# Seven products in both halves of the FFN down columns, two buffers for the weight sums, and PSUM halves copied by ScalarE

## The chip, the cores and the metric

The kernel runs on one core of a Trainium2 chip. The metric is the device time of one execution in microseconds (us). The kernel before takes 1904.34 us, the median of three runs (1903.96 to 1905.06 us).

## The reference, cut to what matters

Two encoder layers over 256 positions of width 2048. Each has a mixing part (projection, dilated attention, pooling, output projection) and a feed-forward part; the change is in the second:

```python
f = jnp.square(jax.nn.relu(rms_norm(x, g_ffn_pre) @ w_up)) @ w_down
return x + rms_norm(f, g_ffn_post)
```

`w_up` is 2048 x 8192, `w_down` 8192 x 2048, all in f32.

## The kernel before

**Products.** TensorE takes fp32r operands, so every f32 operand is split into a high part (a cast, on ScalarE) and a low part (operand minus high part, on VectorE), and a product is three matmuls: high x high, high x low, low x high (`three`, lines 845 to 849, whose three matmuls are L847, L848, L849). ScalarE makes `w_hi` (`split_hi`, L956), VectorE `w_lo` (`split_lo`, L1356). Weights come as 0.5 MB pieces into the four buffers `raw` (SP's queue issues the load of a buffer once its `w_lo` is made), and the split pieces lie in a ring of eight slots (`RING`). A slot is written again after TensorE has used it (`w_used`).

**The FFN.** A layer has four groups `g`, each of 2048 of the 8192 hidden columns: four up units (`turned_unit`, hidden by position, so that the results are already laid out for the down product), then two wide down stages, `j` = 0 for output columns 0 to 1023 and `j` = 1 for 1024 to 2047. The last group of a layer does the second half in two narrow units instead (`unit`). A wide stage goes through 16 blocks of 128 hidden rows, in `K_ORDER`; a block has four products (two halves of the positions t, two halves of the columns c), which add up in the four banks of `acc_pair`.

**Seven products.** In stage `j` = 0 four pairs of blocks (`SEVEN_AT`: blocks 0, 4, 8 and 12) take seven products for eight, by Strassen's scheme (`seven`, L851). It needs sums of quarters of the activations (`s_sum`, `s_hi`, `s_lo`, made while the up units run) and of the weights (`t_sum`, `t_hi`, `t_lo`: in `seven_lo`, L1892, four subtractions of 128x512, two `w_lo`, one `t_lo` of 128x1536, two `w_lo`). Four of the seven results (`ssa_bank`, both `t_bank`, `o_bank`) are shared by several outputs. They add up in PSUM over all four groups and are added to `acc` once in a layer (`combine`, L1921). `t_sum` has one buffer, so that VectorE begins the sums of the next pair when TensorE has used those of this one (`t_used`).

**Moving results.** After a wide stage VectorE adds its four banks to `acc` (`wide_sums`, L1855; L1843 in the first group, L1846 after). After each half of an up unit (`b` = 0 is complete three quarters into the unit, `b` = 1 at its end) VectorE adds the two 256-column halves of a bank (`turned_square`: a reduction at L1822), then does maximum and square (L1827); ScalarE casts `f_hi` (L1248), VectorE makes `f_lo` (L1833).

**Order.** Each engine's instructions run in the order in which the program writes them; the order of VectorE around the down stages is that of `wide_pair` (L1952) and `group` (L1969), the order of ScalarE that of its own `turned_unit` (L1266) and `group` (L1287). TensorE waits for `acc_free` before the first product into a bank, for `lo_made` before a slot, for `t_lo_made` before the products with weight sums.

Of the kernel before, what the change touches and what calls it, by code (L numbers as in the profile page):

```python
# [141 lines left out]
K_ORDER = ((4, 5, 0, 1, 6, 7, 2, 3, 8, 9, 12, 13, 10, 11, 14, 15), tuple(range(2 * RING)))  # L142


def seven_no(l, g, n):

    return (l * FF_GROUPS + g) * len(SEVEN_AT) + n
# [13 lines left out]
def build(nc, x_in, positions, g_mix_pre, w_in, g_attn_out, w_pool, pool_scale, g_pool_out,  # L161
# [16 lines left out]
    x = own("x", [P, T, D])  # L178
# [50 lines left out]
    q_sum = at("q_sum", [P, 4, CH], F32, r_h)  # L229
    raw_side = at("raw_side", [P, RAW, 2 * CH], F32, r_h + 16384)  # L230
    t_hi = at("t_hi", [P, 3, CH], F32R, r_qkv + 12 * CH)
    t_sum = at("t_sum", [P, 3, CH], F32, r_qkv + 24 * CH)
    t_lo = at("t_lo", [P, 3, CH], F32R, r_qkv + 24 * CH)
# [6 lines left out]
    bias = own("bias", [P, T, SEQ])  # L240
    over_count = own("over_count", [P, len(WINDOWS), SEQ])
# [65 lines left out]
    p_copied, q_step = sem("p_copied"), sem("q_step")  # L307
# [60 lines left out]
    with nc.Block() as block:  # L368
# [3 lines left out]
        def _(sp):  # L372
# [33 lines left out]
            def load_wide(l, g, j, hu):  # L406

                for i in range(SLOTS):
                    p = i % PAIRS

                    sp.wait_ge(lo_made, (hu + i // PAIRS) * PAIRS + p + 1)
                    src = w_down[ld(l, 1), ld(g * D + K_ORDER[j][i] * P, P), ld(j * 2 * CH, 2 * CH)]
                    sp.dma_start(raw[:, p, :], src.rearrange("a p c -> p (a c)")
                                 ).then_inc(raw_loaded[p], 16)
# [81 lines left out]
        def _(pe):  # L496
# [163 lines left out]
            for l in range(DEPTH):  # L660
# [190 lines left out]
                def seven(g, n, hu, result):  # L851

                    i = SEVEN_AT[n]
                    no, s0, s1 = seven_no(l, g, n), i % RING, i % RING + 1
                    k0, k1 = K_ORDER[0][i], K_ORDER[0][i + 1]
                    first = n == 0
                    p_first = first and isinstance(g, int) and g == 0
                    p_last = isinstance(g, int) and g == FF_GROUPS - 1 and n == len(SEVEN_AT) - 1
# [3 lines left out]
                    pe.wait_ge(flo_made, l * 32 + g * 8 + k1 // 2 + 1)  # L862
                    pe.wait_ge(s_lo_made, no + 1)
                    pe.wait_ge(lo_made, (hu + i // PAIRS) * PAIRS + 2 + RAW)
                    three(ssa_bank[:, :], sh[:, 2, :], sl[:, 2, :], w_hi[:, s0, right],
                          w_lo[:, s0, right], p_first, p_last)
                    three(t_bank[0][:, :], f_hi[:, k0, early], f_lo[:, k0, early], w_hi[:, s0, left],
                          w_lo[:, s0, left], p_first, p_last).then_inc(w_used, 1)
# [6 lines left out]
                    pe.wait_ge(t_lo_made, no + 1)  # L875
                    three(t_bank[1][:, :], sh[:, 0, :], sl[:, 0, :], t_hi[:, 0, :], t_lo[:, 0, :],
                          p_first, p_last).then_inc(t_used, 1)
                    three(o_bank[:, :], sh[:, 1, :], sl[:, 1, :], t_hi[:, 1, :], t_lo[:, 1, :],
                          p_first, p_last).then_inc(t_used, 1)
                    if first:  # L880
                        pe.wait_ge(acc_free[1], result + 1)
                    three(acc_pair[1][:, 0, :], f_hi[:, k1, late], f_lo[:, k1, late],
                          t_hi[:, 2, :], t_lo[:, 2, :], first, False).then_inc(t_used, 1)

                def down_wide(g, j, hu, result):

                    for i in range(SLOTS):
                        slot, kt = i % RING, K_ORDER[j][i]
# [7 lines left out]
                        for t in range(T):  # L896
                            for c in range(2):
                                if i == 0:
                                    pe.wait_ge(acc_free[t], result + c)
                                begin = i == 0 if j else i == 2 and (t, c) == (1, 1)  # L900
# [1371 lines left out]
```

## Time and profile before

| | |
|---|---|
| median of the runs | 1904.34 us |
| profiled execution, span | 1903.1 us |
| TensorE busy | 1891.0 us, 99% |
| VectorE busy | 1445.1 us, 76% |
| ScalarE busy | 983.1 us, 52% |
| DMA: share of 16 engines, bytes | 62%, 381 MB |
| largest groups of VectorE and ScalarE | `w_lo` 832.3 us, `w_hi` 705.5 us |

The profile is of one execution: its span of 1903.1 us runs from the first to the last instruction, 1.2 us below the median of the runs. A matmul row gives the time until its result has drained, so two neighbours overlap; what a matmul costs TensorE is the distance between two starts. Rows of VectorE and ScalarE overlap a little in the same way.

### The profile page before, as it was taken

How to read it: one execution, taken by the hardware profiler on the slowest of the kernel's cores; microseconds unless marked ns; L12 is line 12 of the kernel's file. 1: busy time of each engine (PE TensorE's matmuls, PEld its weight loads, DVE VectorE, ACT ScalarE, POOL GpSimd, SP SyncE). 2: the span in 40 equal slices, each digit the busy share in tenths (PEclk: the TensorE clock that was granted, in tenths of full speed). 3: DMA queues.
4: the chain of work that ended last, by engine and by line, in shares of the span. 5: the costliest groups of instructions: out<-in, count | busy, mean ns of one | idle time of the engine just before them, and what ended most of it. 6: DMA issues, size and time to landing. Idle time of an engine off the chain costs nothing.

```text
span 1903.1 us, 28366 instructions
## 1 busy us (share of the span) xinstructions
PE 1891.0 (99%) x10022; PEld 1685.3 (89%) x10022; DVE 1445.1 (76%) x1777; ACT 983.1 (52%) x1285; POOL 117.6 (6%) x166
## 2 busy tenths in 40 slices
PE   9999999999999999999999999999999999999998
PEld 7988888988988998898888888889889889989987
DVE  6886768886796688579878757678767966876887
ACT  6455656554445445445554556555544544454443
POOL 3920020000000000000000000200000000000000
PEclk9999999999999999999999999999999999999999
DMA  8665356567558557666576554565766575576563
GB/s 290 203 223 173 118 190 218 181 200 241 183 175 262 178 175 227 215 199 187 210 242 220 180 166 138 183 213 169 234 216 200 187 241 187 172 241 209 184 225 149
DMA packets 168325, 380.79 MB, mean 200 GB/s; under 512 B 11968, under 2 KB 14128, under 8 KB 167728
## 3 DMA queue, kind: packets, MB, share of 16 engines
q1 hardware_dynamic: 167904, 377.58, 61.6%
q10 hardware_dynamic: 336, 2.11, 0.3%
q8 instruction: 49, 0.80, 0.2%
q14 instruction: 36, 0.29, 0.0%
HBM read 377.55 MB, written 2.10 MB: 199 GB/s over the span
## 4 chain that ended last, share of the span: by engine, by line
PE 94%; DVE 3%; DMA 1%; issue 1%; ACT 1%; POOL 0%; DVEq 0%; POOLq 0%; ACTq 0%; SPq 0%
PE acc_pair L548 25%; PE acc_pair L553 13%; PE acc_pair L514 8%; PE acc_pair L848 8%; PE acc_pair L516 8%; PE acc_pair L847 8%; PE acc_pair L515 8%; PE acc_pair L849 8%; DVE w_lo L1356 1%; PE o_bank L766 1%; PE t_bank L849 1%; PE t_bank L848 1%; PE t_bank L847 1%; DVE h_both L1410 1%; DMA raw<-in_w_down 0%
## 5 line engine op out<-in xcount | busy, mean ns | idle before, releaser
L1356 DVE TENSOR_TENSOR w_lo<-raw,w_hi 128x1024 fp32r<-128x1024 f32 x687 | 832.3, 1233 | 251.9 <-ACT w_hi L956 243.2
L956 ACT CAST w_hi<-raw 128x1024 fp32r<-128x1024 f32 x687 | 705.5, 1049 | 503.3 <-DVE raw L1904 119.3
L548 PE MATMUL acc_pair<-h_both,w_hi 128*128 128x512 f32 x2176 | 560.2, 380 | 0.1
L548 PEld LDWEIGHTS acc_pair<-h_both,w_hi 128*128 128x128 f32 x2176 | 371.1, 190 | 30.3 <-ACT proj L1025 0.5
L553 PEld LDWEIGHTS acc_pair<-h_both,w_lo 128*128 128x128 f32 x2176 | 327.4, 190 | 29.1
L553 PE MATMUL acc_pair<-h_both,w_lo 128*128 128x256 f32 x2176 | 330.4, 274 | 0.0
L847 PE MATMUL acc_pair<-w_hi,f_hi 128*128 128x512 f32 x672 | 254.7, 379 | 0.0
L848 PE MATMUL acc_pair<-w_lo,f_hi 128*128 128x512 f32 x672 | 254.7, 379 | 0.0
L849 PE MATMUL acc_pair<-w_hi,f_lo 128*128 128x512 f32 x672 | 254.7, 379 | 0.0
L514 PE MATMUL acc_pair<-w_hi,h_both 128*128 128x512 f32 x444 | 170.5, 384 | 1.7 <-DVE w_lo L1356 1.5
L515 PE MATMUL acc_pair<-w_lo,h_both 128*128 128x512 f32 x444 | 168.3, 379 | 0.0
L516 PE MATMUL acc_pair<-w_hi,h_both 128*128 128x512 f32 x444 | 168.3, 379 | 0.0
L514 PE MATMUL acc_pair<-w_hi,f_hi 128*128 128x512 f32 x384 | 148.2, 386 | 0.2
L1248 ACT CAST f_hi<-act_f 128x512 fp32r<-128x512 f32 x60 | 37.1, 619 | 214.1 <-DVE act_f L1827 214.1
L515 PE MATMUL acc_pair<-w_lo,f_hi 128*128 128x512 f32 x384 | 145.5, 379 | 0.0
L516 PE MATMUL acc_pair<-w_hi,f_lo 128*128 128x512 f32 x384 | 145.5, 379 | 0.0
L849 PEld LDWEIGHTS acc_pair<-w_hi,f_lo 128*128 128x128 f32 x672 | 127.0, 189 | 18.1
L848 PEld LDWEIGHTS acc_pair<-w_lo,f_hi 128*128 128x128 f32 x672 | 127.0, 189 | 18.0
L847 PEld LDWEIGHTS acc_pair<-w_hi,f_hi 128*128 128x128 f32 x672 | 127.0, 189 | 18.0
L1822 DVE TENSOR_REDUCE act_f<-acc_pair 128x512 f32<-128x1024 f32 x60 | 73.3, 1221 | 47.1 <-PE acc_pair L553 46.4
L2084 POOL TENSOR_TENSOR rstd<-mean_sq,minus_half 128x1 f32<-128x1 f32 (+1 forms) x16 | 13.5, 843 | 1421.9 <-DVE ss_post L1371 1149.4
L514 PEld LDWEIGHTS acc_pair<-w_hi,h_both 128*128 128x128 f32 x444 | 83.9, 189 | 16.1 <-issue 3.4
(245 smaller groups left out, 1905.4 us busy)
## 6 DMA issues: line engine op xcount, KB each, us to landing
raw<-in_w_up SPq DMA_DIRECT2D x256, 512.0 KB, 4.5
raw<-in_w_down SPq DMA_DIRECT2D x240, 512.0 KB, 4.9
raw<-in_w_in SPq DMA_DIRECT2D x128, 512.0 KB, 4.7
raw<-in_w_out SPq DMA_DIRECT2D x64, 512.0 KB, 5.4
raw_side<-in_w_down SPq DMA_DIRECT2D x16, 512.0 KB, 7.6
x<-in_x SPq DMA_DIRECT2D x8, 256.0 KB, 7.7
w_pool_s<-in_w_pool SPq DMA_DIRECT2D x2, 1024.0 KB, 7.4
post_row<-in_g_mix_post SPq DMA_DIRECT2D x2, 1024.0 KB, 7.4
```

Source lines behind the costliest of these rows:

```text
L514: pe.matmul(bank[:, :], xh, wh, start=begin and k == 0, stop=False)
L515: pe.matmul(bank[:, :], xh, wl, start=False, stop=False)
L516: mm = pe.matmul(bank[:, :], xl, wh, start=False, stop=end and k == 1)
L548: pe.matmul(acc_pair[b][:, m, :], w_hi[:, slot, col:col + P], x_both.rearrange("p s (a n) -> p s n a", a=2), start=(slot, k) == (0, 0), st ...
L553: mm = pe.matmul(acc_pair[b][:, m, 0:SEQ], w_lo[:, slot, col:col + P], x_hi.rearrange("p (a n) -> p n a", a=2), start=False, stop=(slot, k ...
L847: pe.matmul(bank, xh, in_turn(wh), start=start, stop=False)
L848: pe.matmul(bank, xh, in_turn(wl), start=False, stop=False)
L849: return pe.matmul(bank, xl, in_turn(wh), start=False, stop=stop)
L956: act.copy(w_hi[:, half * PAIRS + p, :], raw[:, p, :]).then_inc(hi_made, 1)
L1248: act.copy(f_part(f_hi, u, b), act_f[:, b, :].rearrange("p (k n) -> p k n", k=2)).then_inc(fhi_made, 1)
L1356: dve.tensor_tensor(w_lo[:, slot, :], src[:, p, :], w_hi[:, slot, :].bitcast(F32), ALU.subtract).then_inc(lo_made, 1)
L1822: dve.tensor_reduce(act_f[:, b, :].rearrange("p (k a n) -> p k a n", k=2, a=2), acc_pair[b][:, :, :].rearrange("p k (s n a) -> p k a n s", ...
```

## The change

- Stage `j` = 1 of the first three groups of a layer also takes seven products at its four pairs (same `K_ORDER`, same activation sums, own weight sums).
- The shared results no longer stay in PSUM: at the end of each wide stage VectorE moves the four shared banks into `kept_sums` in SBUF (`shared_sums`; the first group copies, later ones add), and TensorE's next first `seven` waits for that (`shared_free`). The first `seven` of a stage takes its four shared products first. `combine` is done once for each column half.
- The weight sums have two buffers, used in turn. The second lies over `act_f` and two tables of the mixing part. `kept_sums` lies over `x`. `x` is therefore saved to HBM in the first group of a layer and loaded again in the last (1 MB for each half, on ScalarE's queue), the tables likewise.
- In the up units ScalarE copies the second 256-column half of a bank (`take_half`), VectorE adds the first to it (`turned_sum`), ScalarE does maximum and square in two instructions and casts. At the last up unit VectorE makes the weight sums of the second pair, and the first two slots after them, ahead of `turned_sum(g, 3, 1)`; on ScalarE `take_half(g, 3, 1)` stands ahead of the splits of these two slots.

```diff
+    r_x = region(4 * T * D)
+    x = at("x", [P, T, D], F32, r_x)
+    kept_sums = at("kept_sums", [P, T, SHARED, CH], F32, r_x)
...
+    r_t = ((r_qkv + 12 * CH, r_qkv + 24 * CH), (r_qkv, r_tables))
+    t_hi = [at(f"t_hi{n}", [P, 3, CH], F32R, hi) for n, (hi, _) in enumerate(r_t)]
...
-                def seven(g, n, hu, result):
+                def seven(g, j, n, hu, result):
...
+                    th, tl = t_hi[n % 2], t_lo[n % 2]
...
+                    if first and not (isinstance(g, int) and l + g + j == 0):
+                        pe.wait_ge(shared_free, shared_done(l, g, j))
...
+                    def shared_products():
+
+                        pe.wait_ge(t_lo_made, no + 1)
+                        three(t_bank[1][:, :], sh[:, 0, :], sl[:, 0, :], th[:, 0, :], tl[:, 0, :],
+                              first, end).then_inc(t_used, 1)
+                        three(o_bank[:, :], sh[:, 1, :], sl[:, 1, :], th[:, 1, :], tl[:, 1, :],
+                              first, end).then_inc(t_used, 1)
+
                     if first:
-                        pe.wait_ge(acc_free[0], result + 1)
+                        shared_products()
+                        bank_free(0, 0, j, result)
                     three(acc_pair[0][:, 0, :], f_hi[:, k1, early], f_lo[:, k1, early],
                           w_hi[:, s1, left], w_lo[:, s1, left], first, False)
+                    if first:
+                        bank_free(0, 1, j, result)
                     three(acc_pair[0][:, 1, :], sh[:, 3, :], sl[:, 3, :], w_hi[:, s1, right],
                           w_lo[:, s1, right], first, False).then_inc(w_used, 1)
...
                     if first:
-                        pe.wait_ge(acc_free[1], result + 1)
+                        bank_free(1, 0, j, result)
+                    else:
+                        shared_products()
...
                     for i in range(SLOTS):
...
-                        if j == 0 and i in SEVEN_AT:
-                            seven(g, SEVEN_AT.index(i), hu, result)
-                        if j == 0 and i - i % 2 in SEVEN_AT:
+                        if i in SEVEN_AT:
+                            seven(g, j, SEVEN_AT.index(i), hu, result)
+                        if i - i % 2 in SEVEN_AT:
...
+                def take_half(g, u, b):
...
+                    act.copy(act_f[:, b, :].rearrange("p (k a n) -> p k a n", k=2, a=2),
+                             acc_pair[b][:, :, SEQ:].rearrange("p k (n a) -> p k a n", a=2)
+                             ).then_inc(half_taken, 1)
+
                 def turned_hi(g, u, b):
 
+                    act.wait_ge(acc_free[b], 1 + a0 + ACC_F + g * 8 + u + 1)
+                    act.activation(act_f[:, b, :], act_f[:, b, :], ACT.Relu).then_inc(relu_made, 1)
+                    act.wait_ge(relu_made, turned_no(l, g, u, b) + 1)
+                    act.activation(act_f[:, b, :], act_f[:, b, :], ACT.Square).then_inc(f_ready, 1)
...
+                def sums_hi(g, j, n):
+
+                    no = seven_no(l, g, j, n)
+                    if (j, n) == (0, 1):
+                        act.wait_ge(flo_made, l * 32 + g * 8 + 8)
...
+                    take_half(g, u, 1)
                     if (u, 0) in SEVEN_UNIT:
-                        split_hi(hu + 3, 1, (0, 1, 2))
                         s_rest(g, SEVEN_UNIT.index((u, 0)))
+                    if u < CHUNKS - 1:
                         split_hi(hu + 3, 1, (3,))
-                    elif u < CHUNKS - 1:
-                        split_hi(hu + 3, 1)
+                    else:
+                        act.wait_ge(t_third, seven_no(l, g, 0, 1) + 1)
+                        split_hi(hu + 3, 1, (0, 1))
                     turned_hi(g, u, 1)
...
-                def turned_square(g, u, b):
...
+                def turned_sum(g, u, b):
+
+                    dve.wait_ge(half_taken, turned_no(l, g, u, b) + 1)
+                    z = act_f[:, b, :].rearrange("p (k a n) -> p k a n", k=2, a=2)
+                    dve.tensor_tensor(z, acc_pair[b][:, :, 0:SEQ].rearrange("p k (n a) -> p k a n", a=2),
+                                      z, ALU.add).then_inc(acc_free[b], 1)
...
+                def shared_sums(g, j, first):
...
+                    dve.wait_ge(t_used, 3 * seven_no(l, g, j, len(SEVEN_AT)) - 1)
+                    for k, bank in enumerate((ssa_bank, t_bank[0], t_bank[1], o_bank)):
+                        dst = kept_sums[:, 1 - j, k, :]
+                        if first:
+                            dve.tensor_copy(dst, bank[:, :]).then_inc(shared_free, 1)
+                        else:
+                            dve.tensor_tensor(dst, bank[:, :], dst, ALU.add
+                                              ).then_inc(shared_free, 1)
...
                 def wide_pair(g, j, first, last=False):
...
-                    if j == 0:
-                        seven_lo(g, 2, hu + 2, 0)
-                        seven_lo(g, 3, hu + 3, 1)
-                        split_lo(hu + PAIR_HALVES, 0, (0, 1))
+                    seven_lo(g, j, 2, hu + 2, 0)
+                    seven_lo(g, j, 3, hu + 3, 1)
+                    nxt = hu + PAIR_HALVES
+                    if j == 0 and not last:
+                        weight_sums(g, 1, 0, nxt)
+                        split_lo(nxt, 0, (0, 1))
+                        sums_lo(g, 1, 0)
+                        shared_sums(g, j, first)
+                        split_lo(nxt, 0, (2, 3))
+                        weight_sums(g, 1, 1, nxt + 1)
                         wide_sums(g, j, first)
-                        split_lo(hu + PAIR_HALVES, 0, (2, 3))
-                        split_lo(hu + PAIR_HALVES + 1, 1, src=raw_side if last else raw)
+                        split_lo(nxt + 1, 1, (0, 1))
+                        sums_lo(g, 1, 1)
+                        split_lo(nxt + 1, 1, (2, 3))
+                    elif j == 0:
+                        split_lo(nxt, 0, (0, 1))
+                        shared_sums(g, j, first)
+                        split_lo(nxt, 0, (2,))
+                        wide_sums(g, j, first)
+                        split_lo(nxt, 0, (3,))
+                        split_lo(nxt + 1, 1, src=raw_side)
                     else:
-                        for n in range(PAIR_HALVES - 1):
-                            split_lo(hu + n + 2, n % 2)
-                        split_lo(hu + PAIR_HALVES + 1, 1, (0, 1))
+                        split_lo(nxt, 0, (0, 1))
+                        shared_sums(g, j, first)
+                        split_lo(nxt, 0, (2, 3))
                         wide_sums(g, j, first)
-                        split_lo(hu + PAIR_HALVES + 1, 1, (2, 3))
+                        split_lo(nxt + 1, 1)
...
-                        turned_square(g, u, 1)
+                        if u == CHUNKS - 1:
+                            weight_sums(g, 0, 1, hu + u * 2 + 3)
+                            split_lo(hu + u * 2 + 3, 1, (0, 1))
+                        turned_sum(g, u, 1)
```

## Rows read from the trace of the kernel before

**Rows 1.** Page, busy times and granted clock by fortieths of the span.

```profile
PE 1891.0 (99%) x10022; PEld 1685.3 (89%) x10022; DVE 1445.1 (76%) x1777; ACT 983.1 (52%) x1285; POOL 117.6 (6%) x166
...
PEclk9999999999999999999999999999999999999999
```

**Rows 2.** Waits of TensorE: us in total, times, longest.

```profile
PE o_bank L594 <- POOL ident L2109: 1.8, 1, 1.8
PE acc_pair L514 <- DVE w_lo L1356: 1.5, 4, 0.4
```

**Rows 3.** Stretches (up, wide 0, wide 1): us; busy PE, PEld, DVE, ACT, POOL; clock; DMA.

```profile
458.34:542.18 83.84, 83.84 (x513) 76.99 (x513) 63.43 (x77) 36.47 (x40) 0.00 (x0) 1.00 0.60 188
542.18:581.03 38.85, 38.85 (x182) 34.03 (x181) 34.26 (x37) 21.05 (x21) 0.00 (x0) 1.00 0.61 192
581.03:622.46 41.43, 41.43 (x193) 36.18 (x192) 26.86 (x25) 19.96 (x20) 0.00 (x0) 1.00 0.78 253
```

**Rows 4.** Timeline of TensorE: start, duration; first of wide 0, wide 1, next unit.

```profile
542.18 0.38 PE L847 MATMUL ssa_bank<-w_hi,s_hi 128*128 128x512 f32 x1
...
581.04 0.38 PE L847 MATMUL acc_pair<-w_hi,f_hi 128*128 128x512 f32 x1
...
622.48 1.03 PE L548 MATMUL acc_pair<-h_both,w_hi 128*128 128x512 f32 x4
```

**Rows 5.** Timeline of VectorE, same group: start, duration, instruction, idle before it, releaser.

```profile
542.38 1.22 DVE L1822 TENSOR_REDUCE act_f<-acc_pair 128x512 f32<-128x1024 f32 x1
545.02 0.69 DVE L1833 TENSOR_TENSOR f_lo<-act_f,f_hi 128x512 fp32r<-128x512 f32 x1 [0.69 <-ACT f_hi L1248]
...
555.45 0.69 DVE L1901 TENSOR_TENSOR t_sum<-raw 128x512 f32<-128x512 f32 x1
...
558.38 2.36 DVE L1356 TENSOR_TENSOR w_lo<-raw,w_hi 128x1024 fp32r<-128x1024 f32 x2
560.70 1.76 DVE L1917 TENSOR_TENSOR t_lo<-t_sum,t_hi 128x1536 fp32r<-128x1536 f32 x1
562.38 2.35 DVE L1356 TENSOR_TENSOR w_lo<-raw,w_hi 128x1024 fp32r<-128x1024 f32 x2
565.16 0.69 DVE L1901 TENSOR_TENSOR t_sum<-raw 128x512 f32<-128x512 f32 x1 [0.44 <-PE t_bank L849]
...
574.55 1.23 DVE L1356 TENSOR_TENSOR w_lo<-raw,w_hi 128x1024 fp32r<-128x1024 f32 x1 [0.42 <-ACT w_hi L956]
577.02 1.23 DVE L1356 TENSOR_TENSOR w_lo<-raw,w_hi 128x1024 fp32r<-128x1024 f32 x1 [1.24 <-ACT w_hi L956]
579.29 2.73 DVE L1846 SCALAR_TENSOR_TENSOR acc<-acc_pair,rstd,acc 128x512 f32<-128x512 f32 x4 [1.05 <-PE acc_pair L849]
```

**Rows 6.** Timeline of ScalarE: an older relu and square; same group after.

```profile
317.73 0.60 ACT L1003 ACTIVATE act_f<-acc_pair 128x512 f32<-128x512 f32 x1
318.36 0.63 ACT L1006 ACTIVATE act_f<-act_f 128x512 f32<-128x512 f32 x1
...
544.37 0.62 ACT L1248 CAST f_hi<-act_f 128x512 fp32r<-128x512 f32 x1 [2.81 <-DVE act_f L1827]
...
548.01 2.00 ACT L956 CAST w_hi<-raw 128x1024 fp32r<-128x1024 f32 x2 [2.50 <-DVE raw L1904]
```

**Rows 7.** Last group of layer 0, end of wide 0: VectorE, then TensorE.

```profile
907.14 1.23 DVE L1356 TENSOR_TENSOR w_lo<-raw,w_hi 128x1024 fp32r<-128x1024 f32 x1 [2.92 <-ACT w_hi L956]
908.29 2.72 DVE L1846 SCALAR_TENSOR_TENSOR acc<-acc_pair,rstd,acc 128x512 f32<-128x512 f32 x4
...
909.30 0.38 PE L514 MATMUL acc_pair<-w_hi,f_hi 128*128 128x512 f32 x1
```

**Rows 8.** DMA issues: KB each, median us from issue to landing.

```profile
raw<-in_w_down SPq DMA_DIRECT2D x240, 512.0 KB, 4.9
```

More of the change, by code:

```diff
@@ L849, in three, with bank_free @@
                     return pe.matmul(bank, xl, in_turn(wh), start=False, stop=stop)
-                def seven(g, n, hu, result):
+                def bank_free(t, c, j, result):
+                    pe.wait_ge(acc_free[t], result + (c if j else 1))
+                def seven(g, j, n, hu, result):
                     i = SEVEN_AT[n]
[L854 to L858, printed above, removed]
+                    no, s0, s1 = seven_no(l, g, j, n), i % RING, i % RING + 1
+                    k0, k1 = K_ORDER[i], K_ORDER[i + 1]
+                    first, end = n == 0, n == len(SEVEN_AT) - 1
                     left, right = c_cols(0), c_cols(1)
@@ L864, in seven @@
                     pe.wait_ge(lo_made, (hu + i // PAIRS) * PAIRS + 2 + RAW)
                     three(ssa_bank[:, :], sh[:, 2, :], sl[:, 2, :], w_hi[:, s0, right],
[L866 removed]
+                          w_lo[:, s0, right], first, end)
                     three(t_bank[0][:, :], f_hi[:, k0, early], f_lo[:, k0, early], w_hi[:, s0, left],
[L868 removed]
+                          w_lo[:, s0, left], first, end).then_inc(w_used, 1)
@@ L878, in seven @@
-                    three(o_bank[:, :], sh[:, 1, :], sl[:, 1, :], t_hi[:, 1, :], t_lo[:, 1, :],
-                          p_first, p_last).then_inc(t_used, 1)
                     if first:
-                        pe.wait_ge(acc_free[1], result + 1)
+                        bank_free(1, 0, j, result)
+                    else:
+                        shared_products()
                     three(acc_pair[1][:, 0, :], f_hi[:, k1, late], f_lo[:, k1, late],
-                          t_hi[:, 2, :], t_lo[:, 2, :], first, False).then_inc(t_used, 1)
+                          th[:, 2, :], tl[:, 2, :], first, False).then_inc(t_used, 1)
@@ L897, in down_wide @@
                             for c in range(2):
-                                if i == 0:
-                                    pe.wait_ge(acc_free[t], result + c)
-                                begin = i == 0 if j else i == 2 and (t, c) == (1, 1)
+                                begin = i == 2 and (t, c) == (1, 1)
+                                if begin:
+                                    bank_free(t, c, j, result)
                                 mm = three(acc_pair[t][:, c, :], f_hi[:, kt, h_cols(t)],
@@ L1380, in add_posts @@
                     dve.wait_ge(rstd_ready, l * RS_LAYER + h * (RS_POST1 + T) + t + 1)
+                    if not h and c == 0:
+                        dve.wait_ge(x_back[t], 16 * l)
                     part = acc[:, t, c_cols(c)]
@@ L1915, in seven_lo @@
+                def seven_lo(g, j, n, hu, half):
+                    weight_sums(g, j, n, hu)
                     split_lo(hu, half, (0, 1))
-                    dve.wait_ge(t_hi_made, no + 1)
-                    dve.tensor_tensor(t_lo[:, :, :], t_sum[:, :, :], t_hi[:, :, :].bitcast(F32),
-                                      ALU.subtract).then_inc(t_lo_made, 1)
+                    sums_lo(g, j, n)
                     split_lo(hu, half, (2, 3))
-                def combine(which):
-                    q1, q5, q6, q7 = (q_sum[:, k, :] for k in range(4))
+                def shared_sums(g, j, first):
+                    if first and j == 0:
+                        dve.wait_ge(x_saved, 16 * T * (l + 1))
+                    dve.wait_ge(t_used, 3 * seven_no(l, g, j, len(SEVEN_AT)) - 1)
[3 more added lines that the diff above has]
+                            dve.tensor_copy(dst, bank[:, :]).then_inc(shared_free, 1)
+                        else:
+                            dve.tensor_tensor(dst, bank[:, :], dst, ALU.add
+                                              ).then_inc(shared_free, 1)
@@ L1925, in into, with combine @@
+                def combine(j, which):
+                    q7, q1, q5, q6 = (kept_sums[:, 1 - j, k, :] for k in range(SHARED))
+                    base = 16 * l + 8 * (1 - j)
                     def into(t, c, part):
-                        dst = acc[:, t, c_cols(c)]
-                        dve.scalar_tensor_tensor(dst, part, rstd[:, COL_X2 + t:COL_X2 + t + 1], dst,
+                        dst = halves(acc[:, t, c_cols(2 * j + c)])
+                        dve.scalar_tensor_tensor(dst, put_back(part),
+                                                 rstd[:, COL_X2 + t:COL_X2 + t + 1], dst,
@@ L2013, in group @@
                             turned_unit(u)
+                            if last and u < 2:
+                                combine(1, 2 * u)
+                                combine(1, 2 * u + 1)
                     if first:
```

184 lines of the change are left out of this document (112 added, 72 removed).

## The prediction

> **What bounds the kernel now.** Read the busy times first [rows 1]: TensorE is busy for 99% of the span at a granted clock that is full (2.4 GHz) in all forty slices, VectorE for 76%, ScalarE for 52%. Then TensorE's waits [rows 2]: the longest is 1.8 us at the very start, and for slots of weights it waits 1.5 us in all. So TensorE's matmuls are the time, and whatever removes matmuls shortens it, if the other engines deliver as before. Whether they do is not told by an average of 76%, so the third view is busy time by stretch in one group [rows 3]. In the four up units VectorE is busy 63.4 of 83.8 us, in wide stage 0 (seven products) 34.3 of 38.85, in wide stage 1 (eight products) 26.9 of 41.4. Stage 0 is nearly full on VectorE, and the change makes stage 1 like it. The last views are the timelines of VectorE and ScalarE around stage 0 [rows 5, 6], since the change rewrites their order.
>
> **What it removes.** A wide stage is 16 x 4 x 3 = 192 matmuls with eight products and 4 x 3 = 12 fewer with seven. The stages take 38.85 and 41.43 us [rows 3], 2.58 us apart; by start times they are 38.86 and 41.44 [rows 4]. That is 38.85 / 180 = 0.2158 us a matmul, 0.6475 us for one product of three. Six stages change (three groups in two layers): 6 x 2.58 = **15.5 us less on TensorE**. With nothing else changed the span would be 1903.1 - 15.5 = 1887.6.
>
> The Trainium skill ("TensorE: Matmul & The Clock Gate", section "Back-to-back issue gap") puts 512 columns in a stream of weight loads and matmuls at about 131 ns each, against 216 ns for an isolated one. By its first figure the saving would be an estimated 72 x 0.131 = 9.4 us. The trace, a stream with a weight load for each matmul, disagrees and shows 216.
>
> **What it adds, in sum.** VectorE: 24 more pairs at four subtractions of 0.69 and one `t_lo` of 1.76 [rows 5], 4.5 us each, 108 us; shared sums, 14 stages x 4 x about 0.69, 39 us; 60 reductions of 1.22 become additions (at 0.69, like an f32 operation of this size), and the 60 max-and-square operations of some 0.69 leave, 73 us less. Some 75 to 85 us more, about 80% busy. ScalarE: 60 x (0.60 + 0.63 + 0.63) [rows 6], 112 us, and 24 x 1.5 for `t_hi`, 36 us, about 60%. Averages hide both; what counts is when VectorE reaches the steps that free TensorE's banks.
>
> **The hand-over from wide 0 to wide 1.** Let t = 0 be the start of wide 0, 542.18 in the trace. VectorE's new queue after seven pair 3 is: weight sums of wide 1's pair 0, two `w_lo`, `t_lo`, `shared_sums`, two `w_lo`, weight sums of pair 1, and only then `wide_sums`. TensorE, after the four shared products of its first `seven`, waits for the first of these banks: at 38.85 + 4 x 0.6475 = **41.4**.
>
> Steps in start-to-start distances [rows 5]: weight sums 558.38 - 555.45 less a wait of 0.26 for a load (the gap before the second of them), 2.67; two `w_lo` 2.32; `t_lo` 1.68; two `w_lo` 2.34. A pair is 9.0 us against 9.71 of TensorE time. Where is VectorE at the end of pair 3? Before, at 574.55 - 0.42 = 574.13, t = 31.95. After:
> - TensorE finishes up unit 3 at t = 0; 0.2 later the result can be read [rows 4, 5]. ScalarE copies half (0.60), then casts the first of the two slots (1.05; two take 2.00) [rows 6]: t = 1.85. VectorE's two `w_lo` end at 4.2, `turned_sum` (0.65) at 4.8. Only this frees the `b` = 1 banks, which TensorE wants after six products, at 3.9: a stall of 0.9.
> - ScalarE: relu, square and `f_hi` at about 0.65 each, to 6.8; `f_lo` and `s_lo` to 8.0. `t_hi` waits for `f_lo`, since the second buffer lies over `act_f`: 7.5 to 9.0. `t_lo` 10.7, two `w_lo` 13.0. Before, the same point was 555.45, t = 13.3. What the cheaper `turned_sum` and the sums made ahead gain is lost again in waiting for ScalarE.
> - Two more pairs of 9.0 and one wait of 0.1: 31.1.
>
> Then 2.67 + 2.32 + 1.68 + 2.7 (`shared_sums`, priced as the four bank reads at 579.29, 2.73 together [rows 5]) + 2.34 + 2.67 + 0.75 (first `wide_sums`) = 15.1, so **t = 46.2 against 41.4: a stall of 4.8 us** (the 0.9 is within it, since VectorE waits for none of it). The same from the trace of before alone: `wide_sums` began at t = 37.1 with 2.7 us of idle time since 574.13 (0.42 + 1.24 + 1.05 [rows 5]); taking these out and putting in the 11.7 us of new steps, of which 0.9 was gained earlier, gives 45.2 for its start, and its deadline is 40.7. Bounds: if VectorE never waited after t = 1.85, its steps to the first `wide_sums` sum to 40.4, t = 42.2, a stall of 0.8. Each pair's load must also land in time: a load takes 4.9 us [rows 8] and a buffer comes round again about as fast, so the upper bound has up to 0.5 us at three places, 6.3.
>
> **The hand-over from wide 1 to the next up unit.** `shared_sums` waits for the last shared product, nine products before the end E of the stage: E - 5.83 + 0.2. Four moves 2.7, two `w_lo` 2.3, two of the `wide_sums` 1.4: E + 0.8, while TensorE wants both banks at E. Before, `wide_sums` began 1.75 ahead of the end of a stage (579.29 against 581.04) and nothing waited [rows 4, 5]. VectorE has caught up by then only just, so 0.75 to 1.5; I take 0.9. The up units cover themselves: their `b` = 1 banks are wanted 5.2 us after the unit's end (a quarter of 83.84 / 4) and come free after some 2.6.
>
> **The last group** has no second seven stage. Before, its second `w_lo` came late for want of a load and `wide_sums` followed at 908.29, 1.0 us before TensorE went on [rows 7]. Now 2.7 of `shared_sums` and one `w_lo` of 1.15 stand between, and two banks take 1.4: 913.5 against 909.3, a stall of 4.2. If the load lands early it is about 1.2, with further loads of `x` beside it perhaps 5.
>
> **Sum.** 6 x (4.8 + 0.9) + 2 x 4.2 = 42.6 us of new stalls, 15.5 saved: 27.1 more. On the profiled execution's 1903.1 that is 1930.2; with the 1.2 us by which the median lies above it, **1931.4**. Saving and restoring `x` and the tables (some 9 MB against 381) I take as nothing, hidden under TensorE; if a restored `x` came late it would show at the end of a layer. `combine` for the second half goes into up units with 5 us to spare each on VectorE (63.4 of 83.8 busy), and two ScalarE copies a layer leave; nothing on the path.
>
> **Rivals.**
> - *VectorE arrives in time*, and the change brings its 15.5 us or most of it: 1889 with no stall, 1893 to 1900 with the bounds of 0.8 and 0.75. For it: TensorE never waits now, and the shared products come first so as to leave 2.6 us. The point that decides is t = 40.7 for the start of `wide_sums`; VectorE would have to be 5 us earlier than worked out, which needs nearly all its waits for ScalarE gone. 0.12.
> - *Half as late*: waits overlap better than in my chain, 3 us a group, the last groups' loads land early: 1904.3 - 15.5 + 6 x 3.3 + 2 x 2 = 1912.6. 0.15.
> - *The clock falls too.* Around t = 40 to 46 TensorE idles about 1 and then 3 us with 2.6 us of work between. No row shows TensorE idle for more than 1.8 us [rows 2], with the clock full throughout [rows 1]. If it ran at 1.2 GHz for as long after as it was idle, 1.5 us in each of six groups: 9 more, 1940. 0.15. The Trainium skill ("TensorE: Matmul & The Clock Gate", section "HAM oscillation — how this bites in real kernels") has idle gaps send TensorE back to the slow clock; by that this rival happens wherever the gap is long enough, and no row here shows one.
> - *The forecast*: 0.58.
>
> **Numbers.** Likeliest 1931. The range leaves out the first rival and a little of the second below, and a fallen clock with upper bounds above (6 x 7.8 + 2 x 5 + 9 - 15.5 = 50, 1955): 1906 to 1944. What a measurement of this kernel can tell from no change is 0.2%, 3.8 us. Faster by more: 0.12, the first rival. Within: 0.05, from the second. Slower: the rest, 0.83.
>
> **What would show it.** TensorE's waits, nearly empty now, should hold a wait for `acc` written by VectorE of 3 us or so in six places, one for a shared bank of about 1 us before it, one of about 1 us for `act_f` at each group's wide 0, and one of 4 us in each last group. A group should take 83.8 + 2 x 38.85 + about 5.7 us. VectorE between pair 3 and `wide_sums` should show no idle time; if it does, the chain is wrong. If TensorE's waits stay under 10 us in total, so is the forecast's sign.

## The result and the profile after

The changed kernel takes 1931.51 us, the median of four runs (1928.0 to 1933.03 us); the kernel before takes 1904.41 (four runs). The ratio is 1.0139, 95% interval 1.0125 to 1.0153: 27.1 us slower. The profiled execution is the fastest of the four, 1928.0 us, with a span of 1925.8.

The page of the kernel after (its first lines, and the granted clock by fortieths), beside [rows 1] of before:

```profile
span 1925.8 us, 28908 instructions
...
PE 1883.6 (98%) x9950; PEld 1670.0 (87%) x9950; DVE 1512.7 (79%) x1909; ACT 1112.5 (58%) x1485; POOL 117.7 (6%) x166
...
PEclk9999999999999999999999999999999999999999
```

TensorE has 72 matmuls less (9950 for 10022) and is busy 7.4 us less, in a span 22.7 us longer. VectorE went up by 68 us, to 79%, ScalarE by 129, to 58%. By these shares no engine but TensorE is near its limit, and TensorE has less to do than before.

TensorE's waits say where the time went (columns: us in total, times, longest), where [rows 2] had nothing but the start and 1.5 us for slots:

```profile
PE acc_pair L867 <- DVE acc L1931: 10.4, 4, 2.6
PE acc_pair L867 <- DVE act_f L1908: 5.9, 8, 0.7
PE acc_pair L867 <- DVE acc L1928: 5.2, 2, 2.6
PE ssa_bank L867 <- DVE kept_sums L2028: 3.0, 4, 1.0
PE acc_pair L534 <- DVE acc L1931: 2.1, 2, 1.1
PE acc_pair L568 <- DVE acc L1931: 1.9, 4, 0.5
```

Apart from the start and the slots (1.2 us), which were there before, these are waits for banks that VectorE frees: 15.6 us in six places for the first bank of wide 1 (L1931 and, in a first group, L1928, are `wide_sums`), 5.9 in eight for the last half of the up units (L1908 is `turned_sum`), 3.0 and 0.7 (in first groups, L2026) for the shared banks (L2028), 2.9 in six for the first banks of the next up unit, 2.1 in the two last groups. In all 30 us. A reported wait is counted from the end of the last row, which lies 0.16 us beyond the point where the next matmul would have started; and the distance behind the matmul that waited is 0.1 us longer than usual. So by the distance of two starts each stop costs 0.27 us more than its wait, as the rows of TensorE show (start, duration):

```profile
544.78 0.38 PE L867 MATMUL ssa_bank<-w_hi,s_hi 128*128 128x512 f32 x1
...
549.57 0.48 PE L867 MATMUL acc_pair<-t_hi,f_hi 128*128 128x512 f32 x1 [0.74 <-DVE act_f L1908]
...
585.81 0.48 PE L867 MATMUL ssa_bank<-w_hi,s_hi 128*128 128x512 f32 x1 [1.01 <-DVE kept_sums L2028]
...
588.29 0.38 PE L869 MATMUL o_bank<-t_hi,s_lo 128*128 128x512 f32 x1
591.27 0.48 PE L867 MATMUL acc_pair<-w_hi,f_hi 128*128 128x512 f32 x1 [2.61 <-DVE acc L1931]
591.59 0.38 PE L868 MATMUL acc_pair<-w_lo,f_hi 128*128 128x512 f32 x1
```

From 588.29 to 591.27 it is 2.98 for 0.216, and the next distance 0.32 for 0.216. Together 2.87 us for a wait of 2.61. So the 28 waits cost 30.2 + 28 x 0.27 = 37.8 us. By stretches, the group of [rows 3] (up units, wide 0, wide 1; us, then busy PE, PEld, DVE, ACT, POOL, then clock and DMA):

```profile
460.84:544.79 83.95, 83.95 (x513) 77.15 (x514) 59.11 (x74) 49.51 (x62) 0.00 (x0) 1.00 0.66 209
544.79:585.81 41.02, 39.28 (x182) 33.75 (x181) 36.41 (x41) 24.15 (x25) 0.00 (x0) 1.00 0.58 180
585.81:628.34 42.53, 39.40 (x181) 33.70 (x181) 39.84 (x44) 22.07 (x21) 0.00 (x0) 1.00 0.63 205
```

The group takes 167.50 us; it took 164.12 before, and without stalls it would take 83.84 + 2 x 38.85 = 161.54.

### The profile page after: what moved, and what is told of

Same layout as the page of the kernel before. It is cut to its first block, busy times and chain, and to the rows that moved or that the text cites. A ratio compares the mean times of both kernels' runs of the same rounds, so it can differ in the third digit from the quotient of the medians.

```text
span 1925.8 us, 28908 instructions
## 1 busy us (share of the span) xinstructions
PE 1883.6 (98%) x9950; PEld 1670.0 (87%) x9950; DVE 1512.7 (79%) x1909; ACT 1112.5 (58%) x1485; POOL 117.7 (6%) x166
## 4 chain that ended last, share of the span: by engine, by line
PE 76%; DVE 13%; issue 4%; DMA 4%; ACT 2%; DVEq 0%; POOL 0%; ACTq 0%; POOLq 0%; SPq 0%
PE acc_pair L568 24%; PE acc_pair L573 12%; PE acc_pair L534 8%; PE acc_pair L535 8%; PE acc_pair L536 8%; DVE w_lo L1439 6%; PE acc_pair L867 3%; PE acc_pair L868 3%; PE acc_pair L869 3%; DMA raw<-in_w_down 3%; DVE kept_sums L2028 1%; DVE t_sum L1996 1%; ACT w_hi L991 1%; DVE t_lo L2007 1%; PE o_bank L786 1%
## 5 line engine op out<-in xcount | busy, mean ns | idle before, releaser
L867 PE MATMUL acc_pair<-w_hi,f_hi 128*128 128x512 f32 x504 | 191.9, 381 | 15.6 <-DVE acc L1931 10.4
L868 PE MATMUL acc_pair<-w_lo,f_hi 128*128 128x512 f32 x504 | 191.3, 380 | 0.0
L869 PE MATMUL acc_pair<-w_hi,f_lo 128*128 128x512 f32 x504 | 191.1, 379 | 0.0
L534 PE MATMUL acc_pair<-w_hi,f_hi 128*128 128x512 f32 x384 | 148.2, 386 | 2.1 <-DVE acc L1931 2.1
L535 PE MATMUL acc_pair<-w_lo,f_hi 128*128 128x512 f32 x384 | 145.5, 379 | 0.0
L536 PE MATMUL acc_pair<-w_hi,f_lo 128*128 128x512 f32 x384 | 145.5, 379 | 0.0
L867 PEld LDWEIGHTS acc_pair<-w_hi,f_hi 128*128 128x128 f32 x504 | 95.4, 189 | 31.6 <-DVE acc L1931 12.0
L869 PEld LDWEIGHTS acc_pair<-w_hi,f_lo 128*128 128x128 f32 x504 | 95.4, 189 | 13.6
L868 PEld LDWEIGHTS acc_pair<-w_lo,f_hi 128*128 128x128 f32 x504 | 95.4, 189 | 13.4
L2007 DVE TENSOR_TENSOR t_lo<-t_sum,t_hi 128x1536 fp32r<-128x1536 f32 x56 | 98.2, 1754 | 7.9 <-ACT t_hi L1321 7.9
L1288 ACT COPY act_f<-acc_pair 128x512 f32<-128x512 f32 x60 | 35.0, 584 | 114.3 <-PE acc_pair L573 114.3
```

The costliest lines, as they stand in the source:

```text
L534: pe.matmul(bank[:, :], xh, wh, start=begin and k == 0, stop=False)
L535: pe.matmul(bank[:, :], xh, wl, start=False, stop=False)
L536: mm = pe.matmul(bank[:, :], xl, wh, start=False, stop=end and k == 1)
L867: pe.matmul(bank, xh, in_turn(wh), start=start, stop=False)
L868: pe.matmul(bank, xh, in_turn(wl), start=False, stop=False)
L869: return pe.matmul(bank, xl, in_turn(wh), start=False, stop=stop)
```

## Why it waits: the hand-over on VectorE

VectorE in the same group, wide 0 starting at 544.78, to set beside [rows 5]:

```profile
546.55 2.36 DVE L1439 TENSOR_TENSOR w_lo<-raw,w_hi 128x1024 fp32r<-128x1024 f32 x2
548.83 0.69 DVE L1908 TENSOR_TENSOR act_f<-acc_pair,act_f 128x512 f32<-128x512 f32 x1
551.59 0.69 DVE L1918 TENSOR_TENSOR f_lo<-act_f,f_hi 128x512 fp32r<-128x512 f32 x1 [2.08 <-ACT f_hi L1299]
...
553.90 1.76 DVE L2007 TENSOR_TENSOR t_lo<-t_sum,t_hi 128x1536 fp32r<-128x1536 f32 x1 [1.02 <-ACT t_hi L1321]
...
557.85 0.68 DVE L1989 TENSOR_TENSOR t_sum<-raw 128x512 f32<-128x512 f32 x1
...
566.68 0.68 DVE L1989 TENSOR_TENSOR t_sum<-raw 128x512 f32<-128x512 f32 x1
...
576.11 0.68 DVE L1989 TENSOR_TENSOR t_sum<-raw 128x512 f32<-128x512 f32 x1
...
583.19 0.68 DVE L2028 TENSOR_TENSOR kept_sums<-ssa_bank,kept_sums 128x512 f32<-128x512 f32 x1
...
585.58 2.35 DVE L1439 TENSOR_TENSOR w_lo<-raw,w_hi 128x1024 fp32r<-128x1024 f32 x2
...
590.47 2.72 DVE L1931 SCALAR_TENSOR_TENSOR acc<-acc_pair,rstd,acc 128x512 f32<-128x512 f32 x4
```

And ScalarE, beside [rows 6]:

```profile
544.98 0.59 ACT L1288 COPY act_f<-acc_pair 128x512 f32<-128x512 f32 x1 [1.95 <-PE acc_pair L573]
545.46 1.99 ACT L991 CAST w_hi<-raw 128x1024 fp32r<-128x1024 f32 x2
549.55 0.63 ACT L1295 ACTIVATE act_f<-act_f 128x512 f32<-128x512 f32 x1 [2.09 <-DVE act_f L1908]
...
552.40 1.48 ACT L1321 CAST t_hi<-t_sum 128x1536 fp32r<-128x1536 f32 x1 [0.39 <-DVE f_lo L1918]
```

Read from the top. ScalarE copies its half at t = 0.2 and casts two slots; VectorE's `w_lo` for these (546.55) stand ahead of `turned_sum` (548.83, t = 4.05), and TensorE takes its product at 549.57 after a wait. Then VectorE waits 2.08 for relu, square and cast, and 1.02 for `t_hi`, which ScalarE starts at 552.40, once `f_lo` has left the memory under it. From there VectorE is never idle but for two loads (0.50 and 0.41 us): pair 1 ends at t = 13.1, pair 2 at 21.9, pair 3 at 31.3, `shared_sums` begin at 38.4, `wide_sums` at 45.7. TensorE goes on at 591.27, t = 46.5, with a product that it could have taken at 41.4.

## Experiments

The theory: **VectorE is late**. The steps that free banks stand in its queue behind work that can wait, and it has no spare time there. The rivals: the weight loads set the pace; the detour of the up units through ScalarE is the whole cause; VectorE simply lacks throughput over two wide stages with seven products. All were timed beside the kernel before, which took 1904.8 to 1905.2 us.

### e1: more work ahead of the bank

`added` is a buffer of one column that nothing reads.

```diff
                         weight_sums(g, 1, 1, nxt + 1)
+                        dve.tensor_reduce(added[:, :], acc[:, 0, 2 * CH:4 * CH], AX.X, ALU.add)
                         wide_sums(g, j, first)
```

> The kernel after with one more VectorE operation (a reduction of 128x1024, about 1.22 us, whose result nothing uses) ahead of wide_sums at the end of wide 0, in the six groups that hand over to a wide stage with seven products. Theory 'VectorE is late' (it has no spare time between pair 3 and wide_sums): the wait for the first bank grows from 2.6 to 3.8 us and the time by 6 x 1.2 = 7.3 us, to 1938 to 1941. Rival 'loads' (the weight loads set the pace, VectorE has idle time to absorb it): no change, 1931.

Measured: 1944.32 us, 12.8 more than the kernel after; ratio to before 1.0209 (1.019 to 1.0227). TensorE's waits for the first bank:

```profile
PE acc_pair L868 <- DVE acc L1932: 14.9, 4, 3.7
PE acc_pair L868 <- DVE acc L1929: 7.5, 2, 3.7
```

2.6 has become 3.7 in all six places, 6.8 us together: VectorE has no slack there, and the loads do not set the pace. The other 6 us are more than the theory gives, and the time lies above the range expected. They led to the clock, below: in this trace five of the six wide 1 stages run at a mean granted clock of 0.96 or less (one of 0.93), and the six together take 7.7 us more than in the kernel after.

### e2: the last half of the up units ahead of two slots

```diff
                             weight_sums(g, 0, 1, hu + u * 2 + 3)
-                            split_lo(hu + u * 2 + 3, 1, (0, 1))
                         turned_sum(g, u, 1)
+                        if u == CHUNKS - 1:
+                            split_lo(hu + u * 2 + 3, 1, (0, 1))
```

> The kernel after with turned_sum of the last up unit's second half ahead of the two w_lo of pair 1, not behind them. Theory 'VectorE is late': the step falls into VectorE's wait for ScalarE at t = 1.6 to 1.9, the relu chain starts 2 us earlier, pair 1 ends near t = 11 for 13.9, and all of it is gained at the hand-over: the stall at the start (1.0) goes, the wait for shared banks (0.9) goes, the 2.9 shrinks to about 2; 6 x 2.5 to 2.9 and 2 x 1.0 less, 1912 to 1916, less still if the clock falls less often. Rival 'only the 1.0 us waits count' (the lateness at the hand-over has another cause): 8 us less, 1923.

Measured: 1919.74 us, 11.8 less than after, but 3.7 above the range expected. The eight waits of 0.7 and those for shared banks are gone. Those for the first bank of wide 1 are hardly shorter (1.9 to 2.6 us, in the kernel after 2.6), though VectorE gets there earlier: between the last shared bank and the first other one VectorE has 5.6 us of work (two `w_lo`, weight sums, one `wide_sums`), TensorE 2.6 us. In this group VectorE has freed the last shared bank at 583.10, just as wide 1 begins, so that nearly the whole difference of 3.0 us is a stop. And five of the six wide 1 stages are 1.7 us longer than the sixth. Two of the six, from the end of the stall to the next up unit (the number behind POOL is the granted clock):

```profile
588.71:627.47 38.76, 38.24 (x169) 32.72 (x169) 34.52 (x37) 20.27 (x20) 0.00 (x0) 0.96 0.64 202
755.54:792.52 36.98, 36.55 (x168) 31.51 (x169) 34.42 (x37) 20.16 (x20) 0.00 (x0) 1.00 0.67 211
```

The same work takes 38.76 and 36.98 us, at a mean clock of 0.96 and 1.00.

### e3: the square back on VectorE

The diff is the change's own, undone: `turned_square` for `take_half`, `turned_sum` and the two activations.

```diff
-                def turned_sum(g, u, b):
+                def turned_square(g, u, b):
...
-                        turned_sum(g, u, 1)
+                        turned_square(g, u, 1)
```

> The kernel after with the up units as before the change: VectorE reduces both halves and does maximum and square, ScalarE only casts. Theory 'VectorE is late': VectorE waits less for ScalarE but works 1.2 us longer for each half; the last bank comes free at t = 6.2 for 4.9 (a stall of about 2.5 for 1.0), pair 1 still ends near t = 13.8, so the six hand-overs stay as they are and the two last groups lose 1.5 us each: 1931 to 1936. Rival 'the detour through ScalarE is the cause': the stalls of the six groups mostly go, 1915 or less.

Measured: 1927.49 us (1923.8 to 1931.5), 4 less than after, below the range expected, but with runs that overlap those of the kernel after. `turned_square` stands where `turned_sum` stood, behind the two `w_lo`. TensorE's waits:

```profile
PE acc_pair L867 <- DVE acc L1915: 10.4, 4, 2.6
PE acc_pair L867 <- DVE act_f L1891: 7.6, 8, 1.3
...
PE ssa_bank L867 <- DVE kept_sums L2012: 0.7, 2, 0.4
```

The waits for the first bank of wide 1 are the same 2.6 us; so the detour through ScalarE is not the cause of that stall. It has a share in the smaller ones: the waits for shared banks were 3.7 us and are 0.7, and those in the last groups (2.1) are gone. The start of wide 0 waits 1.0 us on average for 0.7. My price for that, a stall of 2.5, was too high.

### e4: the banks first at the end of wide 0

```diff
                         shared_sums(g, j, first)
+                        wide_sums(g, j, first)
                         split_lo(nxt, 0, (2, 3))
                         weight_sums(g, 1, 1, nxt + 1)
-                        wide_sums(g, j, first)
```

> The kernel after with wide_sums straight behind shared_sums at the end of wide 0, ahead of two w_lo and the weight sums of pair 1. Theory 'VectorE is late' (it lacks time over both wide stages together, not only at one place): the 2.9 us stall at the hand-over goes, but TensorE then runs ahead and the 0.8 us stall at the end of wide 1 grows to about 3.4 with small waits for slots before it: 1926 to 1932. Rival 'only the order at the hand-over is wrong': 6 x 2.9 less and nothing back, 1914.

Measured: 1927.41 us (1924.5 to 1934.3), 4 less than after, again with runs that overlap. The largest of TensorE's waits, at the next up unit, and the second:

```profile
PE acc_pair L568 <- DVE acc L1931: 9.5, 4, 2.9
PE acc_pair L867 <- DVE act_f L1908: 5.9, 8, 0.7
```

No wait for the first bank of wide 1 is left, and the one at the end of wide 1 grew from 0.5 to between 1.8 and 2.9 (L1931 and, in first groups, L1928): 13.9 us for 2.9, where 15.6 have gone. One hand-over put right moves most of the stall to the next. The clock took the rest: with 0.27 us for each stop the stalls are 31.2 us for 37.8, but in this trace the granted clock falls in four of the up units that begin with the new wait, and they take 7.9 us more for it, where the kernel after lost 1.7. The time is in the range expected in part by this term, which the expectation did not hold.

### e8: both hand-overs

e4, and at the end of wide 1:

```diff
-                        split_lo(nxt, 0, (0, 1))
-                        shared_sums(g, j, first)
-                        split_lo(nxt, 0, (2, 3))
+                        split_lo(nxt, 0, (0, 1, 2))
                         wide_sums(g, j, first)
+                        split_lo(nxt, 0, (3,))
+                        shared_sums(g, j, first)
```

> e4 with the end of wide 1 put in order too (three w_lo, wide_sums, the fourth w_lo, then shared_sums), but turned_sum as in after. Theory 'VectorE is late at the steps that free banks': the wait of 1.8 to 2.9 us at the next up unit goes, the 1.0 us at the start of wide 0 and about 1.2 for the shared banks stay, no gap brings the clock down: 1904 to 1909. Rival 'throughput': the waits come back as waits for slots, 1920 or more.

Measured: 1908.78 us, ratio 1.0021 (1.0011 to 1.0031), 22.7 less than after. What is left is mostly what this order does not touch, and 2.0 us in three places at the next up unit, 2.2 in the last groups:

```profile
PE acc_pair L867 <- DVE act_f L1908: 5.9, 8, 0.7
PE ssa_bank L867 <- DVE kept_sums L2028: 3.8, 4, 1.4
```

### e5 and e10: all four places

e8, with `turned_sum` as in e2, and in the last group:

```diff
                         split_lo(nxt, 0, (0, 1))
-                        shared_sums(g, j, first)
-                        split_lo(nxt, 0, (2,))
                         wide_sums(g, j, first)
-                        split_lo(nxt, 0, (3,))
+                        split_lo(nxt, 0, (2, 3))
+                        shared_sums(g, j, first)
```

> The kernel after, same operations, with VectorE's order changed at four places: turned_sum of the last half ahead of two w_lo (as in e2); at the end of wide 0 wide_sums straight behind shared_sums (as in e4); at the end of wide 1 two w_lo, a third, wide_sums, the fourth w_lo, then shared_sums; in the last group wide_sums ahead of the third w_lo and of shared_sums. Theory 'VectorE is late at the steps that free banks': every such step comes in time, stalls of under 0.5 us a group remain, the clock has no cause to fall, and the 15.5 us come through: 1889 to 1894. Rival 'VectorE lacks throughput over the two wide stages' (what e4 gave back): waits for slots take the place, 3 to 4 us in each of six groups, 1908 to 1914.

Measured: 1893.84 us, ratio to before 0.9944 (0.9927 to 0.996). With the same instructions on every engine this is 37.7 us less than the kernel after and 11 less than before. All waits of TensorE that name VectorE in the FFN, with the one for slots that before had too:

```profile
PE acc_pair L534 <- DVE w_lo L1439: 1.2, 3, 0.4
PE acc_pair L534 <- DVE acc L1931: 0.7, 2, 0.4
PE acc_pair L568 <- DVE acc L1928: 0.6, 1, 0.6
...
PE acc_pair L568 <- DVE acc L1931: 0.2, 1, 0.2
```

VectorE at the start of wide 0 (540.85) and at the hand-over:

```profile
542.43 0.68 DVE L1908 TENSOR_TENSOR act_f<-acc_pair,act_f 128x512 f32<-128x512 f32 x1
543.03 2.35 DVE L1439 TENSOR_TENSOR w_lo<-raw,w_hi 128x1024 fp32r<-128x1024 f32 x2
545.47 0.69 DVE L1918 TENSOR_TENSOR f_lo<-act_f,f_hi 128x512 fp32r<-128x512 f32 x1
...
577.06 0.68 DVE L2028 TENSOR_TENSOR kept_sums<-ssa_bank,kept_sums 128x512 f32<-128x512 f32 x1
...
579.46 2.71 DVE L1931 SCALAR_TENSOR_TENSOR acc<-acc_pair,rstd,acc 128x512 f32<-128x512 f32 x4
```

`turned_sum` now stands ahead of the two `w_lo`, `f_lo` follows them with no wait for the cast, and `shared_sums` begin at t = 36.2 for 38.4. VectorE's busy time is that of the kernel after (1511.6 for 1512.7). So throughput was not short: the last rival falls. But nothing is to spare at this hand-over: wide 1 starts at 579.70, just as `shared_sums` have ended.

The kernel ran once more beside e9:

> The same kernel as e5 once more, beside e9 on the same chip: 1892 to 1896, ratio to before 0.993 to 0.996.

Measured: 1893.24 us, ratio 0.994 (0.9923 to 0.9956).

### e9: that order at the hand-overs, with the square on VectorE

The edits of e5 in the wide stages, and the up units of e3. So `turned_square` stands behind the two `w_lo`, where e5 has `turned_sum` ahead of them.

> The order of e5 at the three hand-overs, but the up units as before the change (reduction, maximum and square on VectorE, as in e3). Theory 'VectorE is late': the hand-overs cost nothing any more, but the last bank of the up units comes 1.1 to 1.4 us late in all eight groups, since VectorE reaches its reduction only behind two w_lo, and VectorE has less time to spare in the wide stages: 8 x 1.3 and some small waits over e5, 1904 to 1908. Rival 'ScalarE's part brings nothing': as e5, 1894.

Measured: 1905.45 us, ratio 1.0002 (0.9992 to 1.0011), 12.2 more than e10 on the same chip. Most of it is at the start of wide 0:

```profile
PE acc_pair L867 <- DVE act_f L1891: 7.8, 8, 1.3
```

These waits cost 7.8 + 8 x 0.27 = 10.0 of the 12.2 us. But e5 and e9 differ in two things, in who does relu and square and in the place of the step that frees the last bank, so the 12 us cannot be put down to the first alone. Where both versions stood behind the two `w_lo`, VectorE's was no slower: e3 4 us below the kernel after, e9 3.3 us below e8 (on another chip; e8 also lacks the order of the last group, some 1.4 us). What relu and square on ScalarE are worth in the right order is not shown; it would take e9 with `turned_square` ahead of the two `w_lo`.

### e6: ScalarE's part alone

The kernel before with `take_half`, `turned_sum`, relu and square of the change in its up units, and nothing else.

> The kernel before with only the up units' part of the change (ScalarE copies half, VectorE adds, ScalarE relu, square and cast); turned_sum of the last half at once, seven products in wide 0 alone. Theory 'the detour through ScalarE delays VectorE's next steps': relu, square and cast hold f_lo and s_lo some 1.5 us longer, the weight sums of pair 1 start at t = 5.5 for 4.1, and its first two slots come 1.0 us after TensorE wants them, in all eight groups: 1912 to 1915. Rival 'this part costs nothing by itself': 1905.

Measured: 1906.51 us, ratio 1.0009 (0.9999 to 1.0018), 1.7 more than before. My expectation was wrong. VectorE, with wide 0 starting at 542.17:

```profile
542.99 0.69 DVE L1847 TENSOR_TENSOR act_f<-acc_pair,act_f 128x512 f32<-128x512 f32 x1 [1.77 <-ACT act_f L1259]
545.75 0.69 DVE L1857 TENSOR_TENSOR f_lo<-act_f,f_hi 128x512 fp32r<-128x512 f32 x1 [2.08 <-ACT f_hi L1270]
...
549.55 2.36 DVE L1382 TENSOR_TENSOR w_lo<-raw,w_hi 128x1024 fp32r<-128x1024 f32 x2
```

The bank is read at t = 0.8 and `f_lo` comes at 3.6; the weight sums follow at 4.8, not at 5.5. The first two slots of pair 1 are ready at 551.91, just as TensorE wants them: it starts on them at 551.96, 0.2 us of delay in all. By itself this part costs next to nothing, and brings nothing: VectorE is busy 68 us less than before and the kernel is no faster.

### e7: the gap filled

e2, and in the first `seven` of wide 1:

```diff
                         shared_products()
+                        if j:
+                            pe.wait_ge(none_made, 1)
+                        for k in range(9 if j else 0):
+                            pe.matmul(t_bank[1][:, :], none[:, :].to_broadcast([P, P]),
+                                      w_hi[:, s1, right], start=False, stop=False)
                         bank_free(0, 0, j, result)
```

> e2 with nine more matmuls of 512 columns by zero weights (1.9 us, they add nothing) on TensorE in each of the six gaps of 2.2 to 2.9 us ahead of the first bank of wide 1. The stall itself stays as long. Theory 'the idle time also brings the clock down': in e2's profiled run five of six wide 1 stages were 1.7 us longer than the others; with the gap filled none is, 1919.7 - 5 x 1.7 = 1911, with a mean clock near 1.00. Rival 'the longer stages have another cause': 1920.

`none` is one column of zeros, used as the weights. Measured: 1911.31 us (1909.9 to 1912.1), 8.4 less than e2 with 54 matmuls more; five falls at 1.7 us would be 8.5. The same two stages as above, from the end of the wait:

```profile
587.47:624.54 37.07, 36.55 (x168) 31.52 (x169) 34.49 (x37) 20.16 (x20) 0.00 (x0) 1.00 0.64 209
752.86:789.84 36.98, 36.55 (x168) 31.51 (x169) 34.41 (x37) 20.25 (x20) 0.00 (x0) 1.00 0.68 210
```

Both run at clock 1.00, and the clock falls nowhere else between the kernel's start and its end. The first takes 37.07 us for 38.76. In the kernel after, one wide 1 stage of six was long in the profiled run, the second line here (us; busy PE, PEld, DVE, ACT, POOL; clock, DMA):

```profile
591.27:628.34 37.07, 36.55 (x169) 31.52 (x169) 34.50 (x37) 20.13 (x20) 0.00 (x0) 1.00 0.65 209
1377.92:1416.66 38.74, 38.23 (x168) 32.77 (x169) 34.48 (x37) 20.20 (x19) 0.00 (x0) 0.96 0.64 204
```

The row of the granted clock on the page is too coarse to show this: it has a 9 in every slice.

## Right and wrong, point by point

- **The saving.** 72 matmuls at 0.216: TensorE's spacing is unchanged (rows at 585.81 to 591.59), and e5 shows most of the gain: 11 us of 15.5 by the medians, 13.1 by the spans of the profiled runs (1903.1 and 1890.0). The 2.4 missing there are what e5's own four waits for banks cost, 1.5 + 4 x 0.27 = 2.6.
- **The lateness of VectorE.** This is the mechanism, and it was right. Worked out: `turned_sum` after 4.2, pair 1 at 13.0, pair 3 at 31.1, first bank at 46.2. Measured: 4.05, 13.1, 31.3, and TensorE going on at 46.5. The stalls of a middle group were to be 5.7 us and are 167.50 - 161.54 = 6.0. Over the six groups they are 33 us for 34.2. As forecast, VectorE is never idle between pair 3 and `wide_sums`, which e1 confirms.
- **The last groups** were mis-sized: 4.2 us each, all at the first bank; measured 1.06 + 0.27 = 1.3 there and 1.0 at `turned_sum`, 2.3 together. Two reasons for the 1.9 us: TensorE's first product of the narrow unit waits for one bank of `wide_sums`, not for both as I had counted (0.7), and the load of the second slot was there 1.3 us earlier after wide 0's start than in the kernel before (VectorE's `w_lo` for it at 35.4 us for 36.7). The prediction named the second case itself, with 1.2 us, and chose the other.
- **The clock.** I gave it a chance of 0.15 as a rival, worked out at 1.5 us each time, and left it out of the sum. It happened in part: 1.7 us in one of six places in the profiled run, in five of six in e2's. e7 shows that the idle gap is its cause. The four runs of the kernel after follow it: mean clock 0.998 in the fastest, 0.997 and twice 0.996 in the others, 3.2 to 5 us slower.
- **The match of 1931.4 with 1931.5 is luck.** The sum held 42.6 us of stalls, and the runs show 37.8: 4.8 too much, 3.8 of them in the last groups. It held nothing for the clock. The median run lies 3.5 us above the profiled one, which would be two more falls; with the one seen that is about 5 us (worked out from the 1.7 us of one fall, not seen, since the median run left no trace). The two errors cancel. A small one beside them: the 1.2 us added to a span compares a span with a time, and in every run here that has both, the time is 2.1 to 2.3 us above its own span.
- **Sums that do not come out.** VectorE's added work, 108 + 39 - 73, is 74 us and not 75 to 85; measured 68, and for ScalarE 129 for 148, since rows overlap. The new steps in the second working are 12.1 us by the distances given (2 x 2.67 + 1.68 + 2.7 + 2.34), not 11.7. The bound without waits, 40.4 us and a stall of 0.8, is 41.3 us and 1.7 by the steps listed. The forecast uses none of these; the 1893 to 1900 of the first rival rests on the last.
- **The rival 'VectorE arrives in time'** is what e5 makes true: 1893.8, for 1893 to 1900 worked out. Its condition was named rightly, `wide_sums` begun by t = 40.7 (in e5 at 579.46 - 540.85 = 38.6). It was reached by the order of the queue, not by shorter waits as the prediction had it.
- **Not tried:** the change without the moves of the shared sums; the loads and stores of `x` by themselves (that these cost nothing rests on e5, whose profiled run leaves no part of the expected gain to explain); and relu and square on VectorE with the bank freed first.

## What to carry to other kernels

An in-order engine that serves a full one should run the instruction that frees a buffer before work that is wanted later; here the same instructions in another order were worth 38 us of 1931, some 5 of them (an estimate, from 1.7 us a fall) by way of the clock. Sum the queue from the last point where the serving engine has to wait to each step that the full engine waits for, and compare with the time at which it wants it: the busy share (79%) told nothing. A stall put right at one hand-over may only move to the next (e4), so look at all of them before judging a change.

## What the runs showed of the hardware that I had not expected

TensorE's granted clock can fall behind an idle time of 1.9 to 2.9 us, in some of its occurrences and not in others of the same length. In e2 it fell behind five of six waits (1.9, 2.0 and three of 2.6 us) and not behind one of 2.5; in the kernel after behind one of six of 2.6; in e3's profiled run behind none of six of 2.3 to 2.6; in e4 behind four of six of 1.8 to 2.9; in e1, with waits of 3.7, behind five of six. In e5 and e8, where behind the first microseconds no wait is over 1.4 us, it fell nowhere before the kernel's end. What decides between two waits of the same length no run shows.

A fall goes from 2.4 to 1.2 GHz: from 1379 to 1382 us in the kernel after the granted clock is 0.50, from 1386 on 1.00. The stage behind it has a mean clock of 0.96 and takes 1.7 us longer, more than half of a gap of 2.6 us once more; in one fall of e1 the stage took 2.7 us longer, at 0.93. The Trainium skill ("TensorE: Matmul & The Clock Gate", section "HAM oscillation — how this bites in real kernels") describes such falls behind waits for data in a loop; the trace agrees that a wait brings them, here one for a bank. The Trainium skill's rule there asks for longer gaps than those of e2 and of the kernel after, and by these measurements shorter ones are not safe. Filling the gap with matmuls that add zero removed the falls (e7, 8.4 us), though the stall stayed.
